# The smallest expert group on half-filled tiles: high and low rows in one operand, low down weights on GpSimd

## What is computed

```python
def hierarchical_moe(h, w_rg, b_rg, w_re, b_re, w1, w3, w2):
    ...
    g_val, g_idx = lax.top_k(p_group, 1)            # one of 4 groups for each of 256 tokens
    ...                                             # two of its 4 experts, with weights
    for e in range(N_EXPERTS):                      # 16
        y_e = (jax.nn.silu(t @ w1[e]) * (t @ w3[e])) @ w2[e]
        out = out + combine[:, e:e + 1] * y_e
```

## Time and profile before

| what | value |
|---|---|
| time, median of 3 | 2695.08 us (2693.58 to 2698.35) |
| span of the profiled execution | 2692.0 us |
| busy: TensorE, VectorE, ScalarE, GpSimd | 2642.6 (98%), 1687.4 (63%), 1239.5 (46%), 239.1 (9%) us |
| TensorE's share of the chain that ended last | 92% |
| DMA over the span | 472.33 MB, mean 175 GB/s |
| mean granted TensorE clock | 0.988 of full speed |
| the expert stage | about 2327 to 2688 us of the span |

### The profile page before, as it was taken

One profiled execution on the slowest core, in us unless ns is written; L12 is line 12 of the kernel. 1 busy time (PEld: TensorE's weight loads), 2 busy tenths in 40 slices (PEclk: granted clock), 3 DMA queues, 4 the chain that ended last, 5 costly groups with the idle time before them and its releaser, 6 DMA issues.

```text
span 2692.0 us, 36916 instructions
## 1 busy us (share of the span) xinstructions
PE 2642.6 (98%) x13112; PEld 2087.1 (78%) x13112; DVE 1687.4 (63%) x2560; ACT 1239.5 (46%) x1986; POOL 239.1 (9%) x364
## 2 busy tenths in 40 slices
PE   9999999999998999999999999999999999899999
PEld 7887688888874788888768888885888654688887
DVE  6764577777353777775237777745776552577776
ACT  5444544544333545544235455434543222366565
POOL 0001100100111100001010010012000001000000
PEclk9999999999997999999999999999999999999999
DMA  9542455554331555453255546433553322478885
GB/s 322 195 151 88 179 187 187 184 198 159 104 125 62 216 195 191 157 192 136 94 203 196 187 150 221 166 133 144 193 198 114 112 91 73 156 279 287 310 289 196
DMA packets 337244, 472.33 MB, mean 175 GB/s; under 512 B 15632, under 2 KB 275056, under 8 KB 337152
## 3 DMA queue, kind: packets, MB, share of 16 engines
q1 hardware_dynamic: 334464, 464.02, 48.1%
q0 software_dynamic: 2192, 6.94, 0.8%
q10 hardware_dynamic: 496, 0.17, 0.0%
HBM read 470.01 MB, written 1.10 MB: 175 GB/s over the span
## 4 chain that ended last, share of the span: by engine, by line
PE 92%; DVE 4%; ACT 2%; issue 1%; DMA 1%; POOL 0%; SPq 0%; DVEq 0%; ACTq 0%; POOLq 0%
PE psum_all L1298 22%; PE psum_all L1302 12%; PE psum_all L1423 6%; PE psum_all L1350 6%; PE psum_all L1351 6%; PE psum_all L1352 6%; PE psum_all L1499 4%; PE psum_all L1959 4%; PE psum_all L2919 3%; PE psum_all L2900 3%; PE psum_all L2896 3%; PE psum_all L2897 3%; PE psum_all L1426 2%; PE psum_all L2924 1%; PE psum_all L1444 1%; PE psum_all L1463 1%
## 5 line engine op out<-in xcount | busy, mean ns | idle before, releaser
L1298 PE MATMUL psum_all<-hT_both,gu_hi 128*128 128x512 f32 x2688 | 670.9, 391 | 0.3 <-DVE gu_lo L1136 0.3
L1298 PEld LDWEIGHTS psum_all<-hT_both,gu_hi 128*128 128x128 f32 x2688 | 492.8, 188 | 95.4 <-DVE gu_lo L1136 0.6
L1136 DVE TENSOR_TENSOR gu_lo<-raw_ring,gu_hi 128x2048 fp32r<-128x2048 f32 x176 | 402.0, 2286 | 14.1 <-ACT gu_hi L1124 9.6
L1302 PEld LDWEIGHTS psum_all<-hT_both,gu_lo 128*128 128x128 f32 x2688 | 366.7, 190 | 26.2
L1302 PE MATMUL psum_all<-hT_both,gu_lo 128*128 128x256 f32 x2688 | 374.8, 282 | 0.0
L1124 ACT ACTIVATE gu_hi<-raw_ring 128x2048 fp32r (+1 forms) x175 | 334.2, 1912 | 16.1 <-DVE oT L1635 12.2
L1131 ACT ACTIVATE down_hi<-raw_ring 128x1024 fp32r (+1 forms) x240 | 250.6, 1057 | 137.6 <-PE psum_all L1352 108.6
L1143 DVE TENSOR_TENSOR down_lo<-raw_ring,down_hi 128x1024 fp32r<-128x1024 f32 x240 | 292.4, 1218 | 34.1 <-ACT down_hi L1131 34.1
L1350 PE MATMUL psum_all<-down_hi,hidden_hi 128*128 128x512 f32 x704 | 277.2, 394 | 3.3 <-DVE hidden_lo L1230 2.6
L1351 PE MATMUL psum_all<-down_lo,hidden_hi 128*128 128x512 f32 x704 | 276.0, 392 | 0.0
L1352 PE MATMUL psum_all<-down_hi,hidden_lo 128*128 128x512 f32 x704 | 274.0, 389 | 0.0
(11 more groups left out here) (379 smaller groups left out, 3519.4 us busy)
## 6 DMA issues: line engine op xcount, KB each, us to landing
raw_ring<-in_ffn_w_in SPq DMA_DIRECT2D x174, 1024.0 KB, 7.1
raw_ring<-in_w SPq DMA_DIRECT2D x96, 1024.0 KB, 7.8
raw_ring<-in_ffn_w_out SPq DMA_DIRECT2D x88, 1024.0 KB, 9.1
raw_ring<-in_c_w_in SPq DMA_DIRECT2D x12, 768.0 KB, 5.3
raw_ring<-in_w_in SPq DMA_DIRECT2D x10, 768.0 KB, 6.3
gain<-in_norm_g POOLq DMA_DIRECT2D x12, 512.0 KB, 4.0
raw_ring<-in_a_w_in SPq DMA_DIRECT2D x8, 768.0 KB, 5.3
raw_ring<-in_b_w_in SPq DMA_DIRECT2D x8, 768.0 KB, 5.0
```

The costliest lines, as they stand in the source:

```text
L1136: K.nc.vector.tensor_tensor(K.gu_lo[:, t, :, :], raw_gu(K, slot, t), K.gu_hi[:, t, :, :].bitcast(F32), ALU.subtract).then_inc(K.sem.gu_lo, 1)
L1298: nc.tensor.matmul(out, K.gu_hi[:, t, j, :], K.hT_both[:, k, :, :].rearrange("p c s -> p (c s)"), start=k == 0, stop=False)
L1302: return nc.tensor.matmul(out[:, 0:SEQ], K.gu_lo[:, t, j, :], K.hT_hi[:, k, :], start=False, stop=k == KT - 1)
```

## The change

For T = 4 the tokens' high part takes columns 0 to 63 of the operand's 128 and the low part columns 64 to 127 (`K.hS_hi[:, 2, k, :]`). The last block of places is only 64 wide in the gather (`PLACES` is 576). A gate/up half is then eight matmuls: the packed operand by the high and by the low weights. In PSUM, rows 0 to 63 hold the high tokens' part and rows 64 to 127 the low tokens'. They have to be added: ScalarE copies the lower rows of gate and of up to `K.fold` (partitions 0 to 63), VectorE adds gate and then up into SBUF, the silu reads the added gate, the product the added up. The turn makes 64 columns for each r, the hidden's high and low parts are packed into one operand in the same way, and down is four matmuls by high and four by low weights. The 128 rows of y for T = 4 are added in the scatter, where row p stands for place 512 + p % 64. The low down weights of the slots of T = 4 are made by GpSimd (`pool_experts`); VectorE passes them over and waits in the slot after such a slot until GpSimd is done. The order of the slots stays.

```diff
@@ map_memory
-        self.hS_lo = at("e_tokens_lo", [P, 3, KT, P], self.arena_end + 4 * 3 * D, F32R)
+        self.hS_lo = at("e_tokens_lo", [P, 2, KT, P], self.arena_end + 4 * 3 * D, F32R)
+        self.fold = at("e_fold", [P, 2, PAIR], self.arena_end + 20 * D)
@@ pe_route
-            cols = slice(0, SEQ) if big else slice(SEQ, SLOTS)
+            cols = slice(0, SEQ) if big else slice(SEQ, PLACES)
@@ dve_route (act_route in the same way, with two activations)
+                                       in0=gathered(K, k, False)[:, 0:2 * P].rearrange("p (t s) -> p t s", s=P),
+                                       scalar=gain_col(K, b, k), in1=K.hS_hi[:, 0:2, k, :].bitcast(F32),
+                                       op0=ALU.mult, op1=ALU.subtract)
+        nc.vector.scalar_tensor_tensor(out=K.hS_hi[:, 2, k, FEW:], in0=gathered(K, k, False)[:, 2 * P:],
+                                       scalar=gain_col(K, b, k), in1=K.hS_hi[:, 2, k, 0:FEW].bitcast(F32),
                                        op0=ALU.mult, op1=ALU.subtract).then_inc(K.sem.e_h_lo, 1)
+def pool_experts(K, pool, b):
+
+    T0, F0 = b["tile0"], b["fill0"]
+    for s in b["slots"]:
+        if s["pos"] + 1 != LAST:
+            continue
+        n = s["n"]
+        pool.wait_ge(K.sem.dn_lo, T0 + 2 * n)
+        for r in range(2):
+            pool.wait_ge(K.sem.dn_hi, T0 + 2 * n + r + 1)
+            K.nc.gpsimd.tensor_tensor(K.dn_lo[:, r, :], raw_dn(K, (F0 + n) % RING, r), K.dn_hi[:, r, :].bitcast(F32),
+                                      ALU.subtract).then_inc(K.sem.dn_lo, 1)
@@ act_experts
+    def fold_and_silu(x):
+        u, f = x["u"], folded_before(units, x)
+        if f:
+            act.wait_ge(K.sem.e_fold_gate, 2 * f)
+        for part in range(2):
+            nc.scalar.activation(K.fold[0:FEW, part, :], K.psum[FEW:, 6 + u % 2, part * PAIR:(part + 1) * PAIR], ACT.Copy)\
+                .then_inc(K.sem.e_fold_copy, 1)
+        act.wait_ge(K.sem.e_fold_gate, 2 * f + 1)
+        nc.scalar.activation(K.sg[0:FEW, u % 2, :], K.sg[0:FEW, u % 2, :], ACT.Silu,
+                             scale=K.ws[0:FEW, LAST, 4:5]).then_inc(K.sem.silu, 1)
...
+        if x["T"] == LAST:
+            fold_and_silu(x)
@@ dve_experts
     def down_low(n, r):
+        if n in by_pool:
+            return
+        if n - 1 in by_pool:
+            dve.wait_ge(K.sem.dn_lo, T0 + 2 * n)
         dve_lo_dn(K, dve, r, (F0 + n) % RING, T0 + 2 * n + r + 1)
...
         if more:
             dve_lo_expert(K, dve, b, n + 1, 0)
-        dve.wait_ge(K.sem.silu, T0 + u + 1)
...
+        if x["T"] == LAST:
+            f = folded_before(units, x)
+            for part, dst, src in ((0, K.sg, gate), (1, K.hid, up)):
+                dve.wait_ge(K.sem.e_fold_copy, 2 * f + part + 1)
+                nc.vector.tensor_tensor(dst[rows, u % 2, :], src[rows, :], K.fold[rows, part, :], ALU.add)\
+                    .then_inc(K.sem.e_fold_gate, 1)
+            dve.wait_ge(K.sem.e_fold_gate, 2 * f + 2)
+            up = K.hid[:, u % 2, :]
+        dve.wait_ge(K.sem.silu, T0 + u + 1)
+        nc.vector.scalar_tensor_tensor(out=K.hid[rows, u % 2, :], in0=up[rows, :],
...
@@ pe_experts
+        if x["T"] == LAST:
+            for k in ks:
+                nc.tensor.matmul(out, K.hS_hi[:, 2, k, :], weight(K.ge_hi, k), start=k == 0, stop=False)
+            pe.wait_ge(K.sem.gu_lo, T0 + 2 * n + t + 1)
+            for k in ks:
+                ins = nc.tensor.matmul(out, K.hS_hi[:, 2, k, :], weight(K.ge_lo, k), start=False, stop=k == KT - 1)
+            ins.then_inc(K.sem.e_gu_half if t == 0 else K.sem.gu_done, 1)
+            return
...
         for r in range(2):
-            for hid in (K.hid_hi, K.hid_lo):
+            for hid in (K.hid_hi,) if T == LAST else (K.hid_hi, K.hid_lo):
```

More of the change, by code:

```diff
@@ L64 @@
 SLOTS = 5 * P
+LAST = 4
+FEW = SEQ // 4
+PLACES = LAST * P + FEW
 C_IOTA = C_H_END
@@ L240, in __init__ @@
             some("e_gu_half e_hid_tr e_y_hi e_y_lo")
+        self.e_fold_copy, self.e_fold_gate = some("e_fold_copy e_fold_gate")
         self.chain_act, self.chain_dve, self.out_done = \
@@ L2757, in gate_up_bank, with packed_hidden, few_turned, folded_before @@
     return K.psum[:, 6 + u % 2, 0:PAIR], K.psum[:, 6 + u % 2, PAIR:]
+def packed_hidden(K, u, part):
+    return K.hid_hi[:, u % 2, :].rearrange("p (r s) -> p r s", s=P)[:, :, part * FEW:(part + 1) * FEW]
+def few_turned(K, u):
+    return K.psum[:, 6 + u % 2, 0:SEQ].rearrange("p (r s) -> p r s", s=P)[:, :, 0:FEW]
+def folded_before(units, x):
+    return sum(y["T"] == LAST for y in units[:x["u"]])
 def out_banks(T):
@@ L2799, in act_experts @@
         gate, _ = gate_up_bank(K, u)
-        nc.scalar.activation(K.sg[:, u % 2, :], gate, ACT.Silu,
-                             scale=K.ws[:, x["T"], 4:5]).then_inc(K.sem.silu, 1)
+        if x["T"] == LAST:
+            fold_and_silu(x)
+        else:
+            nc.scalar.activation(K.sg[:, u % 2, :], gate, ACT.Silu,
+                                 scale=K.ws[:, x["T"], 4:5]).then_inc(K.sem.silu, 1)
         if more:
@@ L2851, in dve_experts @@
             dve_lo_expert(K, dve, b, n + 1, 0)
-        dve.wait_ge(K.sem.silu, T0 + u + 1)
         if u >= 2:
             dve.wait_ge(K.sem.e_hid_tr, u - 1)
-        _, up = gate_up_bank(K, u)
-        nc.vector.scalar_tensor_tensor(out=K.hid[:, u % 2, :], in0=up,
-                                       scalar=K.ws[:, x["T"], x["e"]:x["e"] + 1],
-                                       in1=K.sg[:, u % 2, :],
+        rows = slice(0, FEW if x["T"] == LAST else P)
+        gate, up = gate_up_bank(K, u)
+        if x["T"] == LAST:
+            f = folded_before(units, x)
[7 more added lines that the diff above has]
+        nc.vector.scalar_tensor_tensor(out=K.hid[rows, u % 2, :], in0=up[rows, :],
+                                       scalar=K.ws[rows, x["T"], x["e"]:x["e"] + 1],
+                                       in1=K.sg[rows, u % 2, :],
                                        op0=ALU.mult, op1=ALU.mult).then_inc(K.sem.hid_done, 1)
@@ L3139, in _ @@
                     pool_low_x(K, pool, b)
+                    pool_experts(K, pool, b)
                 else:
```

20 lines of the change are left out of this document (15 added, 5 removed).

## The result

The changed kernel takes 2712.4 us (median of 10 runs, 2701.9 to 2715.1), the kernel before beside it 2693.5 (10 runs, 2684.2 to 2699.0): 1.0067 times as long, with an interval of 1.0053 to 1.008. The forecast was 2711 in a range of 2699 to 2722. The profiled run has a span of 2710.2 us, 18.2 more than before, and took 2712.0 as a whole. Executions of one kernel spread over some 15 us, and a part of that lies ahead of the experts: GpSimd's last work ahead of the gather (`pool_low_x`), up to which all kernels of this document have the same code, starts between 2300.2 and 2310.8 us in the profiled executions.

A forecast was written before the change was run, and what follows sets the result against it. TensorE was taken as the bound, the DMA close behind. Span 2692.0 + 14.9 (walk) + 0.4 (gather) + 1 (clock) = 2708.3, plus 3.1 around it: 2711.4, so 2711 us, range 2699 to 2722.

The forecast's parts named there:

- What TensorE is spared: Smallest group's units in the expert stage: 12 matmuls, 2.7 us less each; eight units give 21.7 us, the whole prize.
- The fold: Expert stage: silu waits for VectorE's add behind the next slot's low gate/up; ScalarE's round becomes 9.2 us, hiding TensorE's saving.
- The port: GpSimd and VectorE two-operand SBUF instructions in the expert stage hold each other whole; 9.7 us of work per slot.
- Rival A: Expert stage: the ports hold nobody; the same walk without holds gives +5.2, with the gather 2700.8 us; chance 0.12.
- The walk: Event times from unit 30 to the last down, which ends at 2699.0 instead of 2684.1 us: +14.9 us.
- the tail: Behind the last down: split of y, last scatter, residual and store, 7.9 us to the span's end, unchanged.
- what surrounds the span: Outside the profiled span: median of timed runs lies 3.1 us above it, added to 2708.3 to give 2711.4.
- The step that failed: Expert stage: slot 26's weights land at 2617.2 instead of 2612.1, and ScalarE, in order, waits with all that is queued.
- The gather and the clock: Gather's results cut in two: +0.4 us (-0.3 to +0.8); lower granted clock when TensorE stands still: +1 (0 to +8).
- Rival C: TensorE stays at 1.2 GHz through both runs of smallest-group slots, 1.8 us more eight times: 2725 us; chance 0.12.
- Rival B: Expert stage: ScalarE's round below 8.4 us, TensorE's saving is paid: 2681 with 14 of 21.7 us; chance 0.09.

The follow-up runs named there:

- short_loads: Changed kernel with fills of slots 24 to 31 loading only the first half of each of their three parts; 2708.9 us, 1.0061 to the kernel before.
- low_on_vector: Changed kernel with the low down weights of the smallest group's slots made by VectorE again instead of GpSimd; 2697.2 us, 1.0025 to the kernel before.
- gpsimd_alone: Kernel before with only the low down weights of slots 23 to 26 and 28 to 31 on GpSimd, no packing, no fold; 2693.1 us, 1.0012.
- adds_first_vector: Changed kernel with VectorE's two adds ahead of the next slot's low gate/up and low down weights on VectorE; 2691.1 us, 0.9993 to the kernel before.

## Why the prediction was right, point by point

**What TensorE is spared.** 96 matmuls fewer, right. None of the 21.7 us reached the time.

**The fold.** Silu waits eight times for VectorE, 19.2 us in total: seven times 2.0 us or more (forecast 2.2), and 0.28 at the last unit, behind which there is no slot whose low gate/up could stand in the way. The add takes 0.41 (0.42), the two copies 0.65 (0.76). Right. The kernel with the fold and without GpSimd's part stands at 1.0025, its stage 1.5 us above before: the fold alone takes up all that TensorE is spared.

**The port.** Both of the bounds that I had to choose between are now in rows: GpSimd behind VectorE waits to the end (1.23 us at 2601.76), so does VectorE behind GpSimd, and at GpSimd's change of instruction VectorE gets in. The Trainium skill (SBUF — State Buffer, section "SBUF: two separate sides") says that the one that starts first holds the shared ports for its whole instruction; the trace agrees, in both directions now (7.86 us for a pair that takes 4.64 alone, 1.52 for a product of 0.48). Rival A is out.

**The walk.** All of after's unit 29 is already 1.95 us late (silu at 2588.73 instead of 2586.78). With this taken off, the walk is close in most places; SyncE's issues of slots 26, 27, 28 and 31 in the kernel after:

```profile
2609.79 2.42 SPq L767 DMA_DIRECT2D raw_ring<-in_w  x3
...
2617.94 1.01 SPq L767 DMA_DIRECT2D raw_ring<-in_w  x2
...
2631.87 2.57 SPq L767 DMA_DIRECT2D raw_ring<-in_w  x3
...
2669.43 2.39 SPq L767 DMA_DIRECT2D raw_ring<-in_w  x3
```

Forecast 2608.4, 2615.7, 2633.5 and 2667.1; less the 1.95, measured 2607.8, 2616.0, 2629.9 and 2667.5. Slot 31 was awaited until 2677.64, which makes 2675.7, forecast 2675.6. The one miss among them is slot 28, 3.6 us earlier than forecast: the weights of slot 27 came late (half 0 at 2628.12), so VectorE's low gate/up asked only at 2630.07, during GpSimd's second operation, and didn't get in between the two. It was held itself instead and took 3.78 us instead of 2.29, silu waited 3.50 with it, and by the down of unit 33 the two ways are level again (2644.66 less 1.95, forecast 2642.0). The end of the last down, from the chain of the kernel after (rows of "issue" left out):

```profile
2692.74 1.23 PE psum_all L3009 x4
2694.05 1.07 ACT down_hi L1137
2695.25 2.38 POOL down_lo L2753
2697.62 2.31 POOLq L3156
2699.98 1.19 PE psum_all L3009 x4
2701.17 0.23 PE psum_all L3018
...
2701.75 0.43 PE psum_all L3018
```

2701.17 less 1.95 is 2699.2, forecast 2699.0. So the 18.2 us of the span are 1.95 ahead of the stage, 15.1 in it (forecast 14.9), and 1.1 behind it: the last scatter's matmuls take 0.43 instead of 0.23 after a wait of 2.05 us. I had carried the tail over unchanged.

That 2711 lies so near to 2712.4 is in part luck. The span came out 1.9 us longer than forecast, and the last term of the sum was too large: I took 3.1 us for what surrounds the span, which mixes one execution's span with the median of three times; in the profiled run of the kernel after it is 1.8 (2712.0 less 2710.2).

**The step that failed** isn't in the sum but in its reason. "Slot 26 lands at 2617.2 instead of 2612.1, and ScalarE, in order, waits with all that is queued": I took that wait for part of the price. `short_loads` takes it away, and only 2.4 of the stage's 16.2 us go with it (0.06% by the times). Two loops of nearly the same length pass through the stage. The ring's is the pair of slot 28 (2663.47), its free slot, the fill, half 0, the add, half 1, and the pair of slot 30 (2686.89): 23.4 us for two slots, 11.7 for one. The other is that of the single pair of down tiles, in turns with ScalarE's round, 11.1 in `short_loads`. The walk was right because it held both. What one would have drawn from my text, to help the ring, was wrong.

**The gather and the clock.** Forecast 0.4 and 1. This execution was 0.8 us ahead of that of before when the gather began (2307.69 against 2308.51), so the 1.95 us at unit 29 are 2.8 for the gather and the clock behind it. From 2337 to 2352, before and after:

```profile
2337.00:2352.00 15.00, 11.16 (x47) 9.75 (x48) 6.39 (x22) 6.85 (x10) 0.00 (x0) 0.77 0.39 149
```

```profile
2337.00:2352.00 15.00, 11.52 (x41) 9.96 (x42) 4.89 (x17) 5.65 (x8) 0.00 (x0) 0.66 0.34 129
```

In the same stretch, counted from the start of `pool_low_x`, the mean granted clock is 0.66 in nine of the eleven kernels with the change's gather and 0.77 and 0.89 in the other two; in the three without it, it is 0.77, 0.77 and 0.89. So the low clock mostly lasts longer with the new gather, but not always; what sets it wasn't found. What it costs can be read from `low_on_vector` (0.89), which has the change's gather and reaches the silu of unit 29 277.2 us behind that start, the kernel after (0.66) 281.0: up to 3.9 us. The gather itself costs little: `gpsimd_alone`, with the old gather and the same clock of 0.89, needs 277.3. So its term of 0.4 stands within its bounds, and the clock's term of 1 was too small: with the 1.1 at the end, gather and clock took 3.9 us against the 1.4 of the sum. In the stage itself two of eight units have their last matmuls at the lower clock. Rival C (2725) is out.

**Rival B** would have needed ScalarE's round below 8.4 us. It was 9.0 and more. B's condition, the adds ahead of the low gate/up, was then made in `adds_first_vector`; it gave not 2681 but 2691, since in a run of four the DMA bounds at once and VectorE, at 7.9 us a slot, next. Only with the slots spaced does the time come to 2682.

## What to carry to other kernels

Where the busiest engine is at 98% and is spared work, list the loops of waits that pass through the same stage and their lengths; here they were 8.4 us a slot (TensorE), 8.6 (DMA), and, made by the change, 9 (ScalarE behind VectorE) and over 11 (GpSimd in both), with 7.9 (VectorE, once the adds come first) behind them. Shortening the first gave nothing. Compare traces of two kernels from an event that both have, since one stretch of the span can hold different work in them. When a wait is taken away and the time stays, look which pair of engines meets elsewhere now, and shorten what stands in both loops. Put an instruction that releases another engine ahead of one that only prepares the next step, and work with two SBUF operands not on GpSimd while VectorE has such work in the same loop.

## What the runs showed of the hardware that I had not expected

Two GpSimd operations of 2.33 us take anything between 4.7 and 11.2 us as a pair, by where VectorE's two-operand instructions of 2.29 us fall: they get in between the two, even three in a row. An earlier start can so be lost by the end: counted from the silu of unit 29, GpSimd's third pair came 2.2 us earlier in `short_loads` and ended 0.15 us earlier. The hold also reaches a product with a scalar column, both matrices in SBUF: 1.52 and 1.70 us instead of 0.48 in the kernel after. And behind the gather the granted clock had a mean of 0.66, 0.77 or 0.89 over the same 15 us of work, and two kernels with the same gather differed by up to 3.9 us behind it; why is open.
